# A transformer stack on one core: the gated product turned through memory, the mask in pieces, the mixer's end in another order

## The chip, the cores and the metric

The kernel runs on one core of one Trainium2 chip. The metric is the device time in microseconds (us). The kernel before takes 1723.46 us, the median of three runs (1722.71 to 1724.36).

## The reference

256 tokens of width 1024, all in fp32, pass through four layers. Two layers of the first kind:

```python
x = x + 0.5 * swiglu(rms_norm(x, ffn1_norm[l]), ffn1_w_in[l], ffn1_w_out[l])
x = x + mixer(rms_norm(x, mix_norm[l]), mix_w_in[l], ...)      # attention with a bias table, Fourier mix, two gates
x = x + 0.5 * swiglu(rms_norm(x, ffn2_norm[l]), ffn2_w_in[l], ffn2_w_out[l])
# swiglu: g, u = split(x @ w_in); (silu(g) * u) @ w_out, 2816 wide
```

and, after a norm, two of the second kind: a mixer of four groups (latent attention, short convolution, pooling, sliding-window attention), each group normalised by itself, scaled by `mix_norm` and projected by `w_o`, and then a gated FFN of the same size. There are six FFNs in all. A norm ends the stack. In the first kind's attention a table `rpb` is spread to a bias of 128 x (2 x 8 x 256), to which a mask (0 or -1e30) is added.

## The kernel before, in words

Tokens lie on partitions in two tiles of 128 (`t`). Every large product is done in three fp32r matmuls: both operands are split in a rounded part (`whi`, `xTh`, `bTh`) and a rest (`wlo`, `xTl`, `bTl`), and `product` adds high x high, high x low and low x high. Weights come in units of 1 MB (128 x 2048 fp32) through three slots of `raw`: SP loads a unit in two DMAs (`load`, when VectorE has split what was in the slot), ScalarE rounds it (`refill`, L671), VectorE subtracts (`refill`, L970). Units, steps and layers are counted by semaphores; each engine runs a list of its own, written out by hand, and nothing else orders the work.

An FFN has 11 steps of 256 hidden columns. A step of TensorE is `full_block` (48 matmuls of 512 columns: gate and up of step j+1 into the two banks `pg[1-par]`, weights in slots 2 and 0) and `down` (24 matmuls with the gated product of step j, weights in slot 1, summed in `acc`). ScalarE takes the silu (L701), VectorE multiplies (`product`, L1009) into `act`, tokens on partitions. `down` needs it with hidden columns on partitions: `turn` (L1451), four TensorE transposes into `pg[par][0]` between the two token tiles of `down`, then `product_hi` on ScalarE (L711) and `product_lo` on VectorE (L1019) split the result. VectorE's list for a step is: product_lo, refill slot 1, product of tile 0, refill slot 2, product of tile 1, refill slot 0; ScalarE's has the same order, with silu for the products.

SP's list of an FFN (L462 to L495) loads the first two units, then per step slots 2, 0 and 1. Between chosen steps of a layer's first FFN it issues other loads: the first gain, ahead of step 0; two gains and the constants ahead of step 2; the two gate biases ahead of step 4; the four pieces of the bias table ahead of step 6. GpSimd adds the mask to all of the bias in one instruction (L617) when all four have landed.

In the second kind's mixer (`mixer_b`) TensorE alternates half blocks of the input projection (i = 0 to 7) with small attention products. After the last one come the last attention product, `pair_T(0, 0)` and `pair_T(0, 1)` (transposes of the groups 2 and 3, scaled by VectorE in `scale_pair(0)`, L1287), the first half of the output projection with the convolution in it (`project`, `conv`), and the same for the groups 0 and 1.

Of the kernel before, what the change touches and what calls it, by code (L numbers as in the profile page):

```python
# [20 lines left out]
F32 = mybir.dt.float32  # L21
# [5 lines left out]
P = 128  # L27
# [34 lines left out]
B_IN = 1952  # L62

# [71 lines left out]
class Signals:  # L135

    def __init__(self, sem):
# [37 lines left out]
        self.act_ready = sem("act_ready")  # L176
        self.actT_tr = sem("actT_tr")
# [105 lines left out]
def build(nc, a, out):  # L283

    with ExitStack() as ctx:
# [23 lines left out]
        bTl = sb("bTl", [P, 8, T], F32R)  # L309
        gain_a = sb("gain_a", [P, D])  # L310
# [27 lines left out]
        sg, act = area(12288, TT, FB), area(12800, TT, FB)  # L338
        squared = area(12288, D)
# [47 lines left out]

        spread = nc.dram_tensor("rpb_spread", (GRID_W, DEPTH * NA_H, NA_DR * GRID_W), F32, kind="Internal").ap()
# [29 lines left out]
        def pair_bank(t):  # L418

            return (acc[2], pg[1][0])[t]  # L420
# [17 lines left out]
        def _(sp):  # L438
# [26 lines left out]
            def ffn(w_in, w_out, l, rnd, breaks=((0, None),)):  # L465
                def gate_up(slots, rnds, j):
                    for half in range(2):
                        at = l * (D * 2 * F) + half * (4 * P * 2 * F) + j * FB
# [19 lines left out]
            with sp.Fori(0, DEPTH) as l:  # L488
                (r1, _, _, _), (r2, _, _, _) = ffn_stages_a(l)
# [6 lines left out]
                def gains():  # L496
                    broadcast(gain_m[:, :], "mix_norm", l * D, D, s.gain_m_landed)
                    broadcast(gain_f[:, :], "ffn2_norm", l * D, D, s.gain_f_landed)
                    sp.dma_start(consts_a[:, :], a["consts_a"]).then_inc(s.consts_a_landed, 16)

                def gate_biases():
                    for t in range(TT):
                        broadcast(gate[:, t, :], "mix_gate_bias", l * 2 * D, 2 * D, s.gate_bias_landed)

                def attention_bias():
                    sp.wait_ge(s.rpb_spread, LOADED * NA_DR)
                    for t in range(TT):
                        for r in range(2):
                            first = GRID_H - 1 - (2 * t + r)
                            src = bass.AP(tensor=spread.tensor,  # L510
                                          offset=l * (NA_H * NA_DR * GRID_W) + first * GRID_W,
                                          ap=[[DEPTH * NA_H * NA_DR * GRID_W, GRID_W], [NA_DR * GRID_W, NA_H], [1, T]])
                            sp.dma_start(bias[GRID_W * r:GRID_W * (r + 1), t, :, :], src).then_inc(s.bias_landed, 16)
# [13 lines left out]
                ffn("ffn2_w_in", "ffn2_w_out", l, r2)  # L527
# [6 lines left out]
            with sp.Fori(0, DEPTH) as l:  # L534
# [26 lines left out]
                rf, _, _, _ = ffn_stage_b(l)  # L561
                ffn("w_gate_up_2", "w_down_2", l, rf)
# [15 lines left out]
        def _(pool):  # L578
# [33 lines left out]
            with pool.Fori(0, DEPTH) as l:  # L612
                norm(3 * l)
                pool.wait_ge(s.bias_landed, 64 * l + 64)
                pool.wait_ge(s.consts_a_landed, 16 * l + 16)
# [45 lines left out]
        def _(act_e):  # L661
# [35 lines left out]
            def ffn(rnd, f, n, o):  # L697
# [11 lines left out]
                def product_hi(j, par):  # L709
                    act_e.wait_ge(s.actT_tr, STEPS * f + j + 1)  # L710
                    act_e.activation(bTh[:, 2 * par:2 * par + 2, :], pg[par][0][:, :].rearrange("p (c n) -> p c n", c=2),  # L711
                                     ACT.Copy).then_inc(s.actT_hi, 1)

                with act_e.Fori(0, (STEPS - 1) // 2) as jj:
                    for par in range(2):
                        j = 2 * jj + par
                        product_hi(j, par)
                        refill(1, rnd + j + 1)
                        act_e.wait_ge(s.ffn_t0_done, STEPS * f + j + 2)
                        silu(0, 1 - par)  # L720
# [1174 lines left out]
```

## Time and profile before

| | us |
|---|---|
| median of the timed runs | 1723.46 (1722.71 to 1724.36) |
| span of the profiled execution, first to last instruction | 1721.5 |
| TensorE busy | 1671.8 (97%) |
| VectorE busy | 943.5 (55%) |
| ScalarE busy | 803.8 (47%) |
| GpSimd busy | 97.1 (6%) |
| mean granted TensorE clock | 0.990 of full |

The profile is of one execution. Its own time is the span and what lies around it (the start and end of the program, which the span leaves out); the timed runs are other executions, and their median is 2.0 us over the span. PE is TensorE, DVE is VectorE, ACT is ScalarE, POOL is GpSimd, SP is SyncE, whose only work is to issue DMAs. The granted clock is what share of full speed TensorE was given; 1.0 is 2.4 GHz and 0.5 is 1.2 GHz. A matmul's duration in the rows is longer than its distance to the next, since they are pipelined: distances between starts are what a matmul costs.

### The profile page before, as it was taken

How to read it: one execution, taken by the hardware profiler on the slowest of the kernel's cores; microseconds unless marked ns; L12 is line 12 of the kernel's file. 1: busy time of each engine (PE TensorE's matmuls, PEld its weight loads, DVE VectorE, ACT ScalarE, POOL GpSimd, SP SyncE). 2: the span in 40 equal slices, each digit the busy share in tenths (PEclk: the TensorE clock that was granted, in tenths of full speed). 3: DMA queues.
4: the chain of work that ended last, by engine and by line, in shares of the span. 5: the costliest groups of instructions: out<-in, count | busy, mean ns of one | idle time of the engine just before them, and what ended most of it. 6: DMA issues, size and time to landing. Idle time of an engine off the chain costs nothing.

```text
span 1721.5 us, 22066 instructions
## 1 busy us (share of the span) xinstructions
PE 1671.8 (97%) x7760; PEld 1376.7 (80%) x7760; DVE 943.5 (55%) x843; ACT 803.8 (47%) x899; POOL 97.1 (6%) x105
## 2 busy tenths in 40 slices
PE   6999999999999999999999999899999999999998
PEld 5887887888888787888888888787888878788886
DVE  4545545575545645465566545566554556665454
ACT  5443454544434543444455444465444446544443
POOL 2010000010000002000001000021100002110000
PEclk9999999999999999999999999999999999899999
DMA  8875453446565578555345655644456564336552
GB/s 259 295 221 175 172 190 123 139 156 199 176 208 188 175 251 240 174 173 181 111 152 166 203 188 194 240 127 129 141 190 200 179 195 144 125 127 201 189 192 89
DMA packets 209187, 308.96 MB, mean 179 GB/s; under 512 B 10400, under 2 KB 153504, under 8 KB 208480
## 3 DMA queue, kind: packets, MB, share of 16 engines
q1 hardware_dynamic: 208272, 305.18, 54.1%
q0 software_dynamic: 560, 1.84, 0.4%
q10 hardware_dynamic: 288, 1.05, 0.2%
q8 instruction: 43, 0.70, 0.2%
q14 instruction: 24, 0.20, 0.0%
HBM read 306.97 MB, written 2.88 MB: 180 GB/s over the span
## 4 chain that ended last, share of the span: by engine, by line
PE 90%; DVE 3%; ACT 3%; issue 2%; DMA 1%; POOL 1%; DVEq 0%; SPq 0%; ACTq 0%; POOLq 0%
PE pg L1380 19%; PE pg L1381 18%; PE pg L1382 18%; PE acc L1382 9%; PE acc L1380 9%; PE acc L1381 9%; PE pg L1451 2%; DVE wlo L970 2%; ACT whi L671 1%; DMA raw<-in_ffn_w_in 1%; PE pg L1393 1%; PE acc L1530 1%; PE acc L1550 1%; POOL ms L590 0%; PE acc L1538 0%
## 5 line engine op out<-in xcount | busy, mean ns | idle before, releaser
L970 DVE TENSOR_TENSOR wlo<-raw,whi 128x2048 fp32r<-128x2048 f32 x277 | 641.2, 2316 | 513.8 <-ACT whi L671 513.8
L671 ACT ACTIVATE whi<-raw 128x2048 fp32r<-128x2048 f32 x277 | 529.5, 1913 | 338.6 <-PE pg L1382 168.2
L1380 PE MATMUL pg<-whi,xTh 128*128 128x512 f32 (+1 forms) x1456 | 580.3, 399 | 9.9 <-DVE wlo L970 5.7
L1382 PE MATMUL pg<-whi,xTl 128*128 128x512 f32 (+1 forms) x1456 | 570.4, 392 | 0.0
L1381 PE MATMUL pg<-wlo,xTh 128*128 128x512 f32 (+1 forms) x1456 | 570.2, 392 | 0.0
L1380 PEld LDWEIGHTS pg<-whi,xTh 128*128 128x128 f32 x1456 | 276.3, 190 | 73.6 <-DVE wlo L970 9.8
L1382 PEld LDWEIGHTS pg<-whi,xTl 128*128 128x128 f32 x1456 | 276.0, 190 | 57.5
L1381 PEld LDWEIGHTS pg<-wlo,xTh 128*128 128x128 f32 x1456 | 276.5, 190 | 54.3
L1380 PE MATMUL acc<-whi,bTh 128*128 128x512 f32 (+1 forms) x572 | 229.6, 401 | 0.0
L1382 PE MATMUL acc<-whi,bTl 128*128 128x512 f32 (+1 forms) x572 | 224.3, 392 | 0.0
L1381 PE MATMUL acc<-wlo,bTh 128*128 128x512 f32 (+1 forms) x572 | 223.1, 390 | 0.0
L701 ACT ACTIVATE work<-pg,rstd 128x256 f32<-128x256 f32 x132 | 62.5, 474 | 234.8 <-PE pg L1382 234.7
L1382 PEld LDWEIGHTS acc<-whi,bTl 128*128 128x128 f32 x572 | 107.8, 188 | 23.5
L1381 PEld LDWEIGHTS acc<-wlo,bTh 128*128 128x128 f32 x572 | 108.1, 189 | 20.5
L1380 PEld LDWEIGHTS acc<-whi,bTh 128*128 128x128 f32 x572 | 107.8, 188 | 20.7 <-issue 0.6
L1009 DVE SCALAR_TENSOR_TENSOR work<-pg,rstd,work 128x256 f32<-128x256 f32 x132 | 63.5, 481 | 104.4 <-ACT work L701 104.4
L590 POOL TENSOR_TENSOR ms<-ss,eps 128x1 f32<-128x1 f32 x24 | 25.0, 1041 | 1202.7 <-ACT work L678 1202.6
L711 ACT ACTIVATE bTh<-pg 128x512 fp32r<-128x512 f32 x66 | 39.6, 599 | 83.7 <-PE pg L1451 83.7
L684 ACT ACTIVATE xTh<-pg 128x512 fp32r<-128x512 f32 x48 | 28.4, 597 | 64.6 <-PE pg L1393 64.5
L728 ACT ACTIVATE work<-acc 128x512 f32<-128x512 f32 (+2 forms) x44 | 25.2, 577 | 62.9 <-PE acc L1538 55.0
L1019 DVE TENSOR_TENSOR bTl<-pg,bTh 128x512 fp32r<-128x512 f32 x66 | 45.2, 684 | 15.2 <-ACT bTh L711 15.2
L1393 PE MATMUL pg<-ident,xn 128*128 128x128 f32 x192 | 30.2, 287 | 21.7 <-DVE xn L978 21.7
(159 smaller groups left out, 1048.2 us busy)
## 6 DMA issues: line engine op xcount, KB each, us to landing
raw<-in_ffn_w_in SPq DMA_DIRECT2D x176, 512.0 KB, 4.8
raw<-in_ffn_w_out SPq DMA_DIRECT2D x88, 512.0 KB, 4.0
raw<-in_w_gate_up SPq DMA_DIRECT2D x88, 512.0 KB, 4.7
raw<-in_mix_w_in SPq DMA_DIRECT2D x64, 512.0 KB, 4.1
raw<-in_w_down SPq DMA_DIRECT2D x44, 512.0 KB, 4.0
raw<-in_w_in SPq DMA_DIRECT2D x24, 512.0 KB, 4.8
raw<-in_mix_w_o SPq DMA_DIRECT2D x16, 512.0 KB, 4.7
raw<-in_w_o SPq DMA_DIRECT2D x16, 512.0 KB, 4.5
```

The costliest lines, as they stand in the source:

```text
L671: act_e.activation(whi[:, slot, :], raw[:, slot, :], ACT.Copy).then_inc(s.w_hi_ready, 1)
L684: act_e.activation(xTh[:, 4 * b:4 * b + 4, tok(t)], pg[b][t][:, :].rearrange("p (c n) -> p c n", c=4), ACT.Copy).then_inc(s.xT_hi_ready, 1)
L701: act_e.activation(sg[:, t, :], pg[par][t][:, 0:FB], ACT.Silu, scale=rstd[:, t:t + 1]).then_inc(s.silu_ready, 1)
L711: act_e.activation(bTh[:, 2 * par:2 * par + 2, :], pg[par][0][:, :].rearrange("p (c n) -> p c n", c=2), ACT.Copy).then_inc(s.actT_hi, 1)
L970: v.tensor_tensor(wlo[:, slot, :], raw[:, slot, :], f32(whi[:, slot, :]), ALU.subtract).then_inc(s.w_lo_ready, 1)
L1009: v.scalar_tensor_tensor(act[:, t, :], pg[par][t][:, FB:2 * FB], rstd[:, t:t + 1], sg[:, t, :], ALU.mult, ALU.mult).then_inc(s.act_ready, 1)
L1019: v.tensor_tensor(bTl[:, part, :], pg[par][0][:, :].rearrange("p (c n) -> p c n", c=2), f32(bTh[:, part, :]), ALU.subtract).then_inc(s.act ...
L1380: pe.matmul(dst, xh, wh, start=first and i == 0, stop=False)
L1381: pe.matmul(dst, xh, wl, start=False, stop=False)
L1382: mm = pe.matmul(dst, xl, wh, start=False, stop=last and i == len(pairs) - 1)
L1393: tr = pe.transpose(pg[b][t][:, c * P:(c + 1) * P], xn[:, t, at:at + P], ident[:, :])
L1451: tr = pe.transpose(pg[par][0][:, c * T + t * P:c * T + (t + 1) * P], act[:, t, c * P:(c + 1) * P], ident[:, :])
```

## The change

The gated product of the steps 1 to 9 is no longer turned by TensorE. VectorE transposes `act` in blocks of 32 x 32 within each band of 32 partitions (`turned`), ScalarE's queue stores the result in a DRAM tensor (one DMA, 128 rows of 2 KB), and SP's queue reads it back in four DMAs (32 partitions each, pieces of 512 bytes), so that the bands change places; with the blocks turned and the bands exchanged, `moved` holds the transpose. It is then split from SBUF as it was from PSUM. Steps 0 and 10 keep TensorE's `turn`. On SP the reads of a step stand between the loads of slot 2 and slot 0, and so do the other loads, one per step: first gain in step 0, `gain_m` in 2, constants in 3 (in the first layer only), the bias table's pieces in 4 to 7. The gate biases and `gain_f` are loaded in the mixer instead, and SP's loop over the two layers is written out. GpSimd adds the mask in 16 instructions of 256 columns. In `mixer_b` the end is put in another order: `sw_out(1)` and its square come before the pooling's; `scale_pair` is done per token tile; `pair_T(0, 0)` lies in the last half block and `pair_T(0, 1)` in the first projection, the last attention product behind it; units 13 and 14 are refilled together, ahead of the second pair's split; the first pair uses the banks `pg[1][0]` and `acc[1]`.

```diff
+        turned, moved = area(11264, TT * FB), area(11776, TT * FB)
+        act_blocks = act.rearrange("p t (c b j) -> p b (t c) j", c=2, b=QUADS)
+        turned_blocks = turned.rearrange("p (b n i) -> p b n i", b=QUADS, n=TT * 2)
+        moved_blocks = moved.rearrange("p (a e) -> p a e", a=QUADS)
+        moved_T = moved.rearrange("p (a n i) -> p n a i", a=QUADS, n=TT * 2)
+        stored = nc.dram_tensor("act_blocks", (QUADS, Q, QUADS, TT * FB // QUADS), F32, kind="Internal").ap()
-        def pair_bank(t):
-            return (acc[2], pg[1][0])[t]
+        def pair_bank(k, t):
+            return ((pg[1][0], acc[1]), (acc[2], pg[1][0]))[k][t]
...
@@ SP
+                def move(j):
+                    sp.wait_ge(s.act_stored, 16 * (TURNED * f + j))
+                    for b in range(QUADS):
+                        sp.dma_start(moved_blocks[Q * b:Q * (b + 1)], stored[:, :, b, :].rearrange("a j e -> j a e"))\
+                            .then_inc(s.act_moved, 16)
+                def step(j, moving, extra=None):
+                    def between():
+                        if moving:
+                            move(j - 1)
+                        if extra:
+                            extra()
+                    gate_up((2, 0), (rnd + j, rnd + j + 1), j + 1, between)
+                    down(1, rnd + j + 1, j)
                 gate_up((0, 1), (rnd, rnd), 0)
-                for (begin, other), (end, _) in zip(breaks, (*breaks[1:], (STEPS - 1, None))):
-                    if other:
-                        other()
-                    with sp.Fori(begin, end) as j:
-                        gate_up((2, 0), (rnd + j, rnd + j + 1), j + 1)
-                        down(1, rnd + j + 1, j)
+                for j in range(2):
+                    step(j, False, extras.get(j))
+                for j in range(2, max(extras, default=1) + 1):
+                    step(j, True, extras.get(j))
+                with sp.Fori(max(extras, default=1) + 1, STEPS - 1) as j:
+                    step(j, True)
                 down(2, rnd + STEPS - 1, STEPS - 1)
+                move(STEPS - 2)
...
-                ffn("ffn1_w_in", "ffn1_w_out", l, r1, ((0, gain), (2, gains), (4, gate_biases), (6, attention_bias)))
+                extras = {0: gain, 2: mixer_gain}
+                if l == 0:
+                    extras[3] = constants
+                for i in range(4):
+                    extras[4 + i] = lambda i=i: attention_bias(i // 2, i % 2)
...
                     block_units("mix_w_in", l, A_IN, 0, col, BANK, 2 * b, rm)
+                    if b < 2:
+                        gate_bias(b)
+                    if b == 3:
+                        ffn_gain()
@@ GpSimd
-                flat = bias.rearrange("p t h k -> p (t h) k")
-                pool.tensor_tensor(flat, flat, consts_a[:, CA_MASK:].unsqueeze(1).to_broadcast([P, TT * NA_H, T]),
-                                   ALU.add).then_inc(s.bias_masked, 1)
+                for t in range(TT):
+                    for h in range(NA_H):
+                        pool.tensor_tensor(bias[:, t, h, :], bias[:, t, h, :], consts_a[:, CA_MASK:], ALU.add).then_inc(s.bias_masked, 1)
@@ ScalarE, FFN
+                def moved_hi(j, par):
+                    act_e.wait_ge(s.act_moved, 16 * QUADS * (TURNED * f + j))
+                    act_e.activation(actTh[:, par].rearrange("p n (a i) -> p n a i", a=QUADS), moved_T,
+                                     ACT.Copy).then_inc(s.actT_hi, 1)
+                def store(j):
+                    act_e.wait_ge(s.act_turned, TURNED * f + j)
+                    act_e.dma_start(stored.rearrange("a j b e -> (a j) (b e)"), turned).then_inc(s.act_stored, 16)
...
+                with act_e.Fori(0, (STEPS - 3) // 2) as jj:
+                    for par in (1, 0):
+                        j = 2 * jj + 2 - par
+                        moved_hi(j, par)
+                        step(j, par)
+                        store(j + 1)
@@ ScalarE, mixer_b
                 group_square(0, 3, 0, s.sw_o_sb, 2 * l + 1)
+                group_square(1, 3, 1, s.sw_o_sb, 2 * l + 2)
                 refills(11)
...
                 mla_probs_T(1)
+                group_square(4, 0, 0, s.mla_o_sb, 2 * l + 1)
+                pair_hi(0, 0)
                 mla_exp(2)
                 out_gate_copy(1)
                 mla_probs_T(2)
                 pair_hi(0, 1)
+                refills(12)
...
-                refills(14)
+                refills(13, 14)
                 pair_hi(1, 0)
@@ VectorE, FFN
+                def moved_lo(j, par):
+                    v.wait_ge(s.actT_hi, STEPS * f + j + 1)
+                    hi, lo = (b[:, par].rearrange("p n (a i) -> p n a i", a=QUADS) for b in (actTh, actTl))
+                    v.tensor_tensor(lo, moved_T, f32(hi), ALU.subtract).then_inc(s.actT_lo, 1)
+                def step(j, par, turn=True):
+                    refill(1, rnd + j + 1)
+                    product(0, 1 - par, j + 1)
+                    refill(2, rnd + j + 1)
+                    product(1, 1 - par, j + 1)
+                    if turn:
+                        v.wait_ge(s.act_ready, 2 * STEPS * f + 2 * j + 4)
+                        v.transpose(turned_blocks, act_blocks).then_inc(s.act_turned, 1)
+                    refill(0, rnd + j + 2)
@@ VectorE, mixer_b
                 mla_out(0)
+                sw_out(1)
...
                 refills(11)
-                sw_out(1)
+                v.wait_ge(s.gain_m_landed, 16 * (DEPTH + 1) + 16 * l + 16)
+                scale_pair(0, 0)
                 mla_max(2)
+                scale_pair(0, 1)
+                pair_lo(0, 0)
+                conv_in(1)
+                pair_lo(0, 1)
                 refills(12)
-                conv_in(1)
-                v.wait_ge(s.gain_m_landed, 16 * (DEPTH + 1) + 16 * l + 16)
-                scale_pair(0)
                 mla_out(1)
-                pair_lo(0, 0)
-                pair_lo(0, 1)
-                refills(13)
...
-                scale_pair(1)
-                refills(14)
+                scale_pair(1, 0)
+                scale_pair(1, 1)
+                refills(13, 14)
                 pair_lo(1, 0)
@@ TensorE
-                        if t == 0:
-                            turn(j + 1, 1 - par)
+                        if t == 0 and last:
+                            turn(STEPS - 1, 0)
...
+                                    {0: sw_operands, 7: lambda: pair_T(0, 0)}.get(i))
...
                         mla_attend(0)
+                        sw_attend(2)
                         pool_mix()
...
-                mla_attend(2)
-                pair_T(0, 0)
-                pair_T(0, 1)
-                project(0, 0)
+                project(0, 0, lambda: pair_T(0, 1))
+                mla_attend(2)
                 conv()
                 project(0, 1)
```

## Rows read from the trace of the kernel before

**Rows 1.** The page: an engine's busy time; the chain of waits by engine.
```profile
PE 1671.8 (97%) x7760; PEld 1376.7 (80%) x7760; DVE 943.5 (55%) x843; ACT 803.8 (47%) x899; POOL 97.1 (6%) x105
...
PE 90%; DVE 3%; ACT 3%; issue 2%; DMA 1%; POOL 1%; DVEq 0%; SPq 0%; ACTq 0%; POOLq 0%
```

**Rows 2.** Timeline of TensorE, one step: start, us, line, operation, out<-in, count.
```profile
434.54 0.39 PE L1382 MATMUL pg<-whi,xTl 128*128 128x512 f32 x1
...
437.26 0.40 PE L1382 MATMUL acc<-whi,bTl 128*128 128x512 f32 x1
...
438.17 0.40 PE L1381 MATMUL acc<-wlo,bTh 128*128 128x512 f32 x1
```

**Rows 3.** Timeline of VectorE, same loop; in brackets: idle before, what ended it.
```profile
420.46 2.29 DVE L970 TENSOR_TENSOR wlo<-raw,whi 128x2048 fp32r<-128x2048 f32 x1 [0.40 <-ACT whi L671]
...
434.20 2.29 DVE L970 TENSOR_TENSOR wlo<-raw,whi 128x2048 fp32r<-128x2048 f32 x1 [3.68 <-ACT whi L671]
436.40 0.48 DVE L1009 SCALAR_TENSOR_TENSOR work<-pg,rstd,work 128x256 f32<-128x256 f32 x1
437.28 2.29 DVE L970 TENSOR_TENSOR wlo<-raw,whi 128x2048 fp32r<-128x2048 f32 x1 [0.40 <-ACT whi L671]
```

**Rows 4.** Timeline of ScalarE in the same step.
```profile
438.13 0.60 ACT L711 ACTIVATE bTh<-pg 128x512 fp32r<-128x512 f32 x1 [0.89 <-PE pg L1451]
440.99 1.92 ACT L671 ACTIVATE whi<-raw 128x2048 fp32r<-128x2048 f32 x1 [2.25 <-PE acc L1382]
```

**Rows 5.** Timeline of SP's DMA issues in the same step.
```profile
436.72 4.06 SPq L447 DMA_DIRECT2D raw<-in_ffn_w_in  x4
```

**Rows 6.** DMA issues by transfer: count, KB each, median us to landing.
```profile
raw<-in_ffn_w_in SPq DMA_DIRECT2D x176, 512.0 KB, 4.8
...
x<-in_x ACTq DMA_DIRECT2D x2, 512.0 KB, 4.9
...
out<-xn SPq DMA_DIRECT2D x2, 512.0 KB, 2.6
...
raw<-in_w_ukv SPq DMA_DIRECT2D x4, 128.0 KB, 2.1
```

**Rows 7.** Timelines of GpSimd, VectorE and TensorE at the mask; busy time by window.
```profile
120.87 9.03 POOL L617 TENSOR_TENSOR shared<-shared,consts_a 128x4096 f32<-128x4096 f32 x1 [94.78 <-DMA shared<-rpb_spread]
...
125.93 6.13 DVE L970 TENSOR_TENSOR wlo<-raw,whi 128x2048 fp32r<-128x2048 f32 x1 [3.68 <-ACT whi L671]
...
132.51 0.66 PE L1451 MATMUL pg<-ident,work 128*128 128x128 f32 x4 [3.13 <-DVE work L1009]
...
681.61 0.66 PE L1451 MATMUL pg<-ident,work 128*128 128x128 f32 x4 [2.27 <-DVE work L1009]
...
133.70:137.20 3.50, 3.50 (x10) 2.73 (x9) 1.55 (x2) 0.10 (x1) 0.00 (x0) 0.51 1.02 332
```

**Rows 8.** Timeline of TensorE near the end of the first `mixer_b`.
```profile
1193.14 1.10 PE L1724 MATMUL pg<-work 128*128 128x64 f32 x8 [0.69 <-ACT work L728]
1195.88 1.11 PE L1837 MATMUL acc<-ident,xn 128*128 128x128 f32 x4 [1.63 <-DVE xn L1287]
...
1198.48 0.79 PE L1380 MATMUL pg<-whi,xTh 128*128 128x512 f32 x1 [0.63 <-DVE xTl L1295]
...
1203.02 3.62 PE L1764 MATMUL pg<-work,shared 128*128 128x256 f32 x16
```

**Rows 9.** Timelines of SP and VectorE at the kernel's start; busy time by window.
```profile
1.26 2.27 SPq L447 DMA_DIRECT2D raw<-in_ffn_w_in  x4
3.71 0.93 SPq L455 DMA_DIRECT2D gain_a<-in_ffn_norm  x1
5.06 8.31 SPq L447 DMA_DIRECT2D raw<-in_ffn_w_in  x4
...
12.42 1.29 DVE L978 TENSOR_TENSOR xn<-x,gain_a 128x512 f32<-128x512 f32 x2 [0.19 <-DMA gain_a<-in_ffn_norm]
...
7.00:12.30 5.30, 0.00 (x0) 0.00 (x0) 2.29 (x1) 4.27 (x3) 0.72 (x1) 1.00 1.07 367
```

More of the change, by code:

```diff
@@ L62 @@
 B_IN = 1952
+Q = 32
+QUADS = P // Q
+TURNED = STEPS - 2
 FFN_ROUNDS = STEPS
@@ L309, in build @@
         bTl = sb("bTl", [P, 8, T], F32R)
+        actTh, actTl = (b[:, 0:4, :].rearrange("p (r c) (t i) -> p r (c t) i", r=2, t=TT) for b in (bTh, bTl))
         gain_a = sb("gain_a", [P, D])
@@ L463, in block_units, with ffn, gate_up @@
                          [rows(name, at + 2 * u * P * pitch, pitch, i % SLOTS, 2 * u * n, 2, n) for u in range(2)])
-            def ffn(w_in, w_out, l, rnd, breaks=((0, None),)):
-                def gate_up(slots, rnds, j):
+            def ffn(w_in, w_out, l, rnd, f, extras={}):
+                def gate_up(slots, rnds, j, between=None):
                     for half in range(2):
+                        if half == 1 and between:
+                            between()
                         at = l * (D * 2 * F) + half * (4 * P * 2 * F) + j * FB
@@ L727, in copy @@
+                product_hi(0, pg[0][0])
+                step(0, 0)
+                store(1)
+                with act_e.Fori(0, (STEPS - 3) // 2) as jj:
[4 more added lines that the diff above has]
+                        store(j + 1)
+                moved_hi(STEPS - 2, 1)
+                step(STEPS - 2, 1)
+                product_hi(1, pg[0][0])
             def copy(dst, src, sem, scale=1.0):
@@ L1450, in turn, with down @@
                         for c in range(2):
-                            tr = pe.transpose(pg[par][0][:, c * T + t * P:c * T + (t + 1) * P], act[:, t, c * P:(c + 1) * P], ident[:, :])
+                            tr = pe.transpose(pg[par][0][:, (2 * t + c) * P:(2 * t + c + 1) * P], act[:, t, c * P:(c + 1) * P], ident[:, :])
                     tr.then_inc(s.actT_tr, 1)
                 def added(t, par, slot, n2, k, first, last):
-                    return product(acc[2 * t + n2][:, :], [(bTh[:, 2 * par + k, tok(t)], bTl[:, 2 * par + k, tok(t)],
+                    return product(acc[2 * t + n2][:, :], [(actTh[:, par, 2 * t + k, :], actTl[:, par, 2 * t + k, :],
                                                             *weights(slot, k * D + n2 * BANK, BANK))], first=first, last=last)
-                def down(j, par, slot, r, first):
+                def down(j, par, slot, r, first, last):
                     pe.wait_ge(s.actT_lo, STEPS * f + j + 1)
@@ L1484, in last_down, with step @@
                                     transposes(0, n2, o + 1)
-                def step(j, par, amid=None, first=False):
+                def step(j, par, amid=None, first=False, last=False):
                     full_block((2, 0), (rnd + j, rnd + j + 1), BANK, pg[1 - par], s.ffn_t0_done, amid=amid)
-                    down(j, par, 1, rnd + j + 1, first)
+                    down(j, par, 1, rnd + j + 1, first, last)
                 step(0, 0, {(0, 1): lambda: turn(0, 0)}, first=True)
@@ L1493, in ffn @@
                     step(2 * jj + 2, 0)
-                step(STEPS - 2, 1)
+                step(STEPS - 2, 1, last=True)
                 last_down(2, rnd + STEPS - 1)
@@ L1786, in pool_mix, with pair_T @@
                     mm.then_inc(s.unit_done, 1)
+                def pair_T(k, t):
+                    half = 1 - k
+                    if k == 0 and t == 0:
+                        pe.wait_ge(s.z_ready, 2 * l + 1)
+                        pe.wait_ge(s.out_gate_sb, 2 * l + 1)
+                    if k == 0 and t == 1:
+                        pe.wait_ge(s.sw_biased, 3 * l + 3)
+                    pe.wait_ge(xn_ready[t], 2 * (o + 1) + k + 2)
+                    for c in range(4):
+                        at = (4 * half + c) * P
+                        tr = pe.transpose(pair_bank(k, t)[:, c * P:(c + 1) * P], xn[:, t, at:at + P], ident[:, :])
+                    tr.then_inc(s.tr_done, 1)
                 for i in range(8):
@@ L1825, in mixer_b @@
                         mla_probs_T(2)
-                mla_attend(2)
-                def pair_T(k, t):
-                    half = 1 - k
-                    if k == 0 and t == 1:
-                        pe.wait_ge(s.z_ready, 2 * l + 1)
-                        pe.wait_ge(s.out_gate_sb, 2 * l + 1)
-                    pe.wait_ge(xn_ready[t], 2 * (o + 1) + k + 2)
-                    for c in range(4):
-                        at = (4 * half + c) * P
-                        tr = pe.transpose(pair_bank(t)[:, c * P:(c + 1) * P], xn[:, t, at:at + P], ident[:, :])
-                    tr.then_inc(s.tr_done, 1)
                 def project(i, t, amid=None):
```

124 lines of the change are left out of this document (57 added, 67 removed).

## The prediction

> **What bounds the kernel now.** I read first the page's busy shares and its chain of waits [rows 1]: TensorE is busy for 1671.8 of 1721.5 us and carries 90% of the chain that ended last. So a part of the change can only gain by taking work off TensorE, or by filling one of the places where TensorE stands idle or runs at half clock; and it can only lose by making TensorE wait. Then the timeline of one step of an FFN loop. 66 of these steps (11 in each of 6 FFNs) make up two thirds of the span. VectorE's splits of the same slot lie 16.82 us apart (420.46 and 437.28) [rows 3]; that is the period. TensorE's 72 large matmuls in it (48 for gate and up, 24 for down) follow each other by 0.2267 us (12 of them from 434.54 to 437.26) [rows 2], 16.32 us in all. What is left, 0.50 us, is the four transposes of the gated product: from 437.26 to 438.17 pass 0.91 us for two matmuls and four transposes, 0.46 more than two matmuls [rows 2]; the other 0.04 is spread over the matmuls behind them. No engine makes TensorE wait in this loop. Last I looked for TensorE's idle places: beside the start there are two where the mask is added [rows 7] and one near each end of the second block's two mixers [rows 8].
>
> **The change, part by part.** The profile's span is 1721.5 us; the median of the timed runs, 1723.46, is 2.0 above it. I take the changes from the span and add these 2.0, so they come off the median as they are.
>
> *Transposes removed.* Products 1 to 9 of each FFN go through memory, 0 and 10 stay on TensorE: 9 x 6 = 54 of 66 turns go. 54 x 0.50 = 27.0 us, if the way through memory is hidden.
>
> *Is it hidden?* The step becomes a ring that must close within 16.32 us: VectorE's product of token tile 1, block transpose, store, four reads, ScalarE's rounding copy, ScalarE's split of slot 1 (which stands behind that copy in its order and so waits for the reads), VectorE's split of slot 1, product of tile 0, split of slot 2, and then the next product of tile 1. Its terms:
> - product 0.48 [rows 3].
> - block transpose of 128x512: no such row; two VectorE operations of 512 elements take 1.29 [rows 9], one of 256 takes 0.48 [rows 3]; so between 0.5 and, at two passes, 1.4; I take 0.7.
> - store of 256 KB on ACT's queue: 512 KB of output land in 2.6 with nothing beside them, 512 KB of x on this same queue in 4.9 beside weight loads [rows 6]. The store runs beside the load of slot 2, issued at the same moment [rows 5]; between 2.0 and 4.9, I take 3.0.
> - SP wakes 0.23 after what it waits for (434.20 + 2.29 = 436.49 [rows 3], issue at 436.72 [rows 5]).
> - four reads of 64 KB: four issues took 2.27 in a row [rows 9], so the last is issued 1.7 after the first and lands 2.1 later, as the 128 KB loads do [rows 6]: 3.8; at worst, behind what is left of slot 2's megabyte in the same queue, 6.5.
> - rounding copy 0.60, split on ScalarE 1.92 [rows 4], two splits of 2.29 and a product of 0.48 on VectorE [rows 3], each beginning some 0.09 before the end of the one ahead: 7.2.
> - semaphores between engines, about 0.2.
> Sum 0.48 + 0.7 + 3.0 + 0.23 + 3.8 + 7.2 + 0.2 = 15.6, with 14.4 and 20.9 as ends. So 0.7 us are spare, and TensorE alone should set a period of 16.32. Its own deadline is later still: it needs slot 1 split when the down matmuls begin, some 1.3 us after VectorE is through, and that is spent once in an FFN, not in each step; a ring of up to 16.46 would cost nothing over nine steps.
>
> A rule of the Trainium skill speaks against it: DMA: Bandwidth & Descriptors, section on the anatomy of one DMA, says that a transfer's fixed cost is mostly the wait for the receipt of the last write, and that this is longest when the target is HBM; its latency table gives HBM 0.2 us on average and 2 us at high load. The one store in this trace lands fast, but with no other traffic [rows 6]; beside traffic no row shows a store. By the rows the store's term is 3.0 and the ring 15.6; by the rule at high load it would be some 5 and the ring 17.6, 0.8 over the period before.
>
> *What waits behind the new waits.* On ScalarE the wait for the reads holds up the split of slot 1 and the silu of tile 0, and VectorE waits for both: that is the ring. On SP the wait for the store holds up the loads of slots 0 and 1. VectorE's transpose stands ahead of the split of slot 0, which then ends 0.7 us later; TensorE needs it only at the second half of the next block, over 3 us after 439.57 [rows 3], so nothing. SP's load of slot 0 now stands behind its wait for the store and four issues: it is issued about 6 us after the product instead of 3.4, and lands about 4.8 us after that [rows 6], where ScalarE wants it at 15.3; 4 us spare, less in the four steps that also load a bias piece. The extra traffic, 0.5 MB beside 3 MB in a step, needs 3.5 MB in 16.3 us, 215 GB/s, where 367 GB/s have been moved [rows 9]. Cost nothing; without that cover the same 54 steps pay for it.
>
> *Mask in pieces.* One GpSimd addition of 4096 elements takes 9.03 us, and VectorE's split of 2.29 that meets it takes 6.13 [rows 7]: they exclude each other. TensorE stands for 3.13, and then runs 8 matmuls at 0.427 instead of 0.227 while the clock is at half (the window 133.70 to 137.20 shows 0.51, 1.2 GHz, after that idle place), 1.6 us; in the other layer 2.27 [rows 7]. Together 7.0. A piece of 256 elements should take 9.03/16 = 0.56, with some overhead 0.7, and holds one split by at most that. The 16 pieces reach over one step or a bit more, two splits of the ring in it: up to 1.4 us against 0.7 + 1.3 spare. I take 0.5 per layer as lost: gain 6.0, between 3 and 7.
>
> *Mixer end.* In each of two layers TensorE waits 0.69 for the last probabilities, 1.63 for the scaled pair and 0.63 for its split, then works at half clock: 12 matmuls from 1198.48 to 1203.02 take 4.54 where 2.72 are needed, and the eight transposes lose some 0.8 [rows 8]. 2.95 + 1.8 + 0.8 = 5.6 per layer. Now the pair's squares and scaling come before the last scores, its transposes lie inside matmul blocks, and the last attention follows the first projection. Following the new orders with the durations of rows 3, 4 and 8, the first projection finds its operand about 0.3 us ahead. But the second pair's split now stands behind two weight splits of 2.29 on VectorE, and TensorE then waits about 1.1 there. 5.6 - 1.1 = 4.5 per layer, 9.0 for two; between 0 (a new idle place brings the half clock back) and 12.
>
> *Loads moved.* Only one lies bare: at the start the gain of the first norm was issued at 3.71, ahead of slot 2's megabyte at 5.06; now it is behind it in the same queue. VectorE's first use, at 12.42, waited for exactly this load [rows 9]. A megabyte at the 367 GB/s of that stretch [rows 9] is 2.9 us; x's second half and the bias table's loads share the engines then, so I take 3.7, between 2.5 and 5, and TensorE's whole start shifts by it. In the second layer the same gain lands some 4 us before it is wanted. Gate biases and constants move to where the queue has room: nothing.
>
> Sum: -27.0 - 6.0 - 9.0 + 3.7 = -38.3; 1723.5 - 38.3 = 1685.
>
> **Rivals.**
> A. *The ring is a bit too long*, between 16.46 and 17.0: the reads queue behind slot 2's load. For it: that load's landings and the reads fall together; 0.7 is not much. Against: each term was taken in company. At 16.8 TensorE's saving is given back wholly: 1685 + 27 = 1712.
> B. *The trip through memory decides* (the other side): store and reads together take 2.5 us longer than the 7.0 I gave them, as x's 4.9 in rows 6 and reads at their worst would have it. The ring is 18.1, each of 54 steps loses 1.3 against before: +70, with the other parts 1723.5 + 70 - 11.3, and less what the first steps of each FFN have spare (some 6 x 1.3 = 8): 1774. It decides from a ring of 17.0 on: there 54 x 0.2 = 11 eat the other gains. For it: 2.0 to 4.9 for the store. Against: 4.9 was measured for twice the bytes. The section of the Trainium skill named above would have the store go this way.
> C. *Only the transposes count*: the mixer end gives nothing, since TensorE meets the new idle place and the half clock again, and the mask in pieces costs as much as whole: 1723.5 - 27 + 3.7 = 1700. For it: the reordered work is the same on VectorE and ScalarE. Against: the waits that go are covered by matmuls that exist.
>
> **How the numbers follow.** Forecast 0.60 (1676 to 1694), A 0.12, B 0.16, C 0.12. The range that holds 8 in 10 leaves out B and a little below: 1675 to 1716. No change means within 0.2%, 3.4 us, about what a measurement of this kernel can tell. Faster: forecast, C and most of A, less a little for a ring near 17: 0.82. Same 0.03. Slower 0.15.
>
> **What would show it.** In the changed profile: period between two splits of a slot 16.3 (16.8 or more under A, 18 under B); before ScalarE's rounding copy a wait of some 6 us for the reads, and none of TensorE for the split of slot 1; VectorE's new operation near 0.7; the store landing about 3.0 after issue, the last read about 3.8 after the first; GpSimd with 16 short additions a layer and TensorE without an idle place there; VectorE's first use of the gain near 16 instead of 12.42; near the mixers' end one wait of about 1 us in place of three, and no stretch at half clock. The forecast is wrong if TensorE waits in the loop each step, or if the start does not move.

## The result: 34.5 us slower, and the profile after

The changed kernel takes 1757.6 us (median of four runs, 1756.5 to 1758.8) against 1723.1 of the kernel before on the same chip (1720.7 to 1724.4): 1.0200 times as long, with a 95% interval of 1.0186 to 1.0215. I had forecast 1685, with 1675 to 1716 as range. The span of the profiled execution is 1756.8, 35.3 more than before.

The page of the profile after, busy times, the chain of waits, and two of the DMA issues:

```profile
PE 1661.1 (95%) x7544; PEld 1352.2 (77%) x7544; DVE 966.6 (55%) x897; ACT 782.7 (45%) x899; POOL 113.6 (6%) x135
PE 37%; DMA 24%; DVE 14%; issue 10%; ACT 8%; SPq 4%; POOL 1%; ACTq 0%; DVEq 0%; POOLq 0%
...
act_blocks<-work ACTq DMA_DIRECT2D x54, 256.0 KB, 5.5
work<-act_blocks SPq DMA_DIRECT2D x216, 64.0 KB, 2.0
```

TensorE has 216 instructions less, as meant (54 x 4), and is busy for 10.7 us less. But the chain that ended last, 90% TensorE before [rows 1], is 37% TensorE now. The rest runs through the store, the reads, SP, ScalarE and VectorE: the ring of the prediction has become what bounds the loop. The waits name its places (engine and line, what it waited for: us in total, times, longest):

```profile
ACT bTh L758 <- DMA work<-act_blocks: 551.6, 54, 11.6
DVE bTl L1084 <- ACT bTh L758: 400.1, 54, 8.3
PE acc L1455 <- DVE wlo L1030: 43.8, 50, 1.8
```

ScalarE's wait for the reads would harm nobody by itself. The third row does: TensorE waits 50 times for VectorE's split of slot 1, and that split stands behind the moved product.

One turn of the ring, from the timelines of VectorE, ScalarE, SP and TensorE (start, us, line, operation; idle before in brackets):

```profile
443.29 0.48 DVE L1069 SCALAR_TENSOR_TENSOR work<-pg,rstd,work 128x256 f32<-128x256 f32 x1
443.56 0.95 SPq L462 DMA_DIRECT2D raw<-in_ffn_w_in  x2
443.81 0.71 DVE L1094 STREAM_TRANSPOSE work<-work 128x512 f32<-128x512 f32 x1
444.55 0.33 ACTq L773 DMA_DIRECT2D act_blocks<-work  x1
450.04 1.76 SPq L499 DMA_DIRECT2D work<-act_blocks  x4
453.44 0.63 ACT L758 ACTIVATE bTh<-work 128x512 fp32r<-128x512 f32 x1 [10.66 <-DMA work<-act_blocks]
453.98 1.90 ACT L714 ACTIVATE whi<-raw 128x2048 fp32r<-128x2048 f32 x1
455.92 2.29 DVE L1030 TENSOR_TENSOR wlo<-raw,whi 128x2048 fp32r<-128x2048 f32 x1 [1.11 <-ACT whi L714]
458.26 0.50 PE L1455 MATMUL acc<-whi,bTh 128*128 128x512 f32 x1 [0.81 <-DVE wlo L1030]
460.72 0.48 DVE L1069 SCALAR_TENSOR_TENSOR work<-pg,rstd,work 128x256 f32<-128x256 f32 x1
461.23 0.71 DVE L1094 STREAM_TRANSPOSE work<-work 128x512 f32<-128x512 f32 x1
```

From one block transpose to the next are 17.42 us, where the period before was 16.82 and I had forecast a ring of 15.6. The terms, forecast and measured: product 0.48 and 0.52; transpose 0.7 and 0.74; **store 3.0 and 5.49** (444.55 to 450.04, the issue of the reads included, so 0.23 of waking is in it); reads 3.8 and 3.40; from the copy to the next product 7.2 and 7.28. Only the store is far off: with SP's waking on both sides 3.23 were forecast and 5.49 measured, 2.3 us more. It also lies above the upper end that I had kept, 4.9.

I read the rest from TensorE's timeline, by the starts of the first and the last turn on TensorE (steps 0 and 10) in each of the six FFNs. In us, with the experiments told below:

```
stretch                  before   after   turns on TensorE  split first  combined  loop written out
start to first turn       35.13   37.81       38.85            37.52       34.20       34.55
FFN 1 (mask)             166.23  167.87      161.40           156.87      156.90      156.90
FFN 2                    161.40  167.40      161.27           156.88      156.88      156.90
layer 1 to layer 2        29.84   34.36       31.38            32.99       33.79       28.90
FFN 3 (mask)             163.80  166.53      161.38           156.90      156.90      156.90
FFN 4                    161.40  166.65      161.38           156.88      156.88      156.90
first mixer_b            141.64  146.01      138.90           146.06      138.10      138.90
FFN 5                    161.38  166.65      161.38           156.87      156.87      156.88
second mixer_b           138.46  136.06      135.08           134.62      133.68      133.95
FFN 6                    161.26  166.29      161.38           156.88      156.88      156.87
```

(The mixers of the first kind, 192.5 in all columns, and the end, 16.0, are left out.) An FFN without the mask takes 161.38 before. The six loops together take 1001.4 after against 6 x 161.38 = 968.3: the ring costs 33.1. The mask's stalls, 7.2 in the two loops that had them, are gone. The start costs 2.7 (this stretch moves by itself: 35.13, 34.98 and 33.69 in three profiles in which nothing was changed there), the passage to the second layer 4.5, the first `mixer_b` 4.4; the second gives 2.4 back. 33.1 - 7.2 + 2.7 + 4.5 + 4.4 - 2.4 = 35.1 of the 35.3.

### The profile page after: what moved, and what is told of

Read it like the earlier page. It is cut to its first block, busy times and chain, and to the rows that moved or that the text cites. A ratio compares the mean times of both kernels' runs of the same rounds, so it can differ in the third digit from the quotient of the medians.

```text
span 1756.8 us, 21384 instructions
## 1 busy us (share of the span) xinstructions
PE 1661.1 (95%) x7544; PEld 1352.2 (77%) x7544; DVE 966.6 (55%) x897; ACT 782.7 (45%) x899; POOL 113.6 (6%) x135
## 4 chain that ended last, share of the span: by engine, by line
PE 37%; DMA 24%; DVE 14%; issue 10%; ACT 8%; SPq 4%; POOL 1%; ACTq 0%; DVEq 0%; POOLq 0%
DMA act_blocks<-work 17%; DVE wlo L1030 8%; PE pg L1455 8%; PE pg L1457 7%; PE pg L1456 7%; ACT whi L714 7%; DMA work<-act_blocks 6%; SPq L499 4%; PE acc L1455 3%; PE acc L1457 3%; PE acc L1456 3%; DVE work L1069 2%; DVE work L1094 2%; PE pg L1468 1%; PE acc L1605 1%
## 5 line engine op out<-in xcount | busy, mean ns | idle before, releaser
L1030 DVE TENSOR_TENSOR wlo<-raw,whi 128x2048 fp32r<-128x2048 f32 x277 | 632.4, 2284 | 204.9 <-ACT whi L714 204.9
L758 ACT ACTIVATE bTh<-work 128x512 fp32r<-128x512 f32 x54 | 34.1, 632 | 551.6 <-DMA work<-act_blocks 551.6
L1084 DVE TENSOR_TENSOR bTl<-work,bTh 128x512 fp32r<-128x512 f32 x54 | 40.2, 745 | 400.1 <-ACT bTh L758 400.1
```

What stands on the lines that cost most here:

```text
L758: act_e.activation(actTh[:, par].rearrange("p n (a i) -> p n a i", a=QUADS), moved_T, ACT.Copy).then_inc(s.actT_hi, 1)
L1030: v.tensor_tensor(wlo[:, slot, :], raw[:, slot, :], f32(whi[:, slot, :]), ALU.subtract).then_inc(s.w_lo_ready, 1)
L1084: v.tensor_tensor(lo, moved_T, f32(hi), ALU.subtract).then_inc(s.actT_lo, 1)
```

## Experiments: what the ring costs, and where it can be opened

**All but the way through memory.** The changed kernel with `turn`, `product_hi` and `product_lo` of the kernel before, and without the block transpose, the store and the reads:

```diff
-                        moved_hi(j, par)
+                        product_hi(j, par)
...
-                        if t == 0 and last:
-                            turn(STEPS - 1, 0)
+                        if t == 0:
+                            turn(j + 1, 1 - par)
```

> The changed kernel with the gated product turned by TensorE again in every step, as before; mask in pieces, spread loads, mixer end and the other load order stay. Theory (the trip through memory is what costs: period 17.43 instead of 16.82): all six FFN loops are back at 161.4 us from the first to the last turn, the two idle places at the mask stay away (-7), the mixer end keeps its 8, the late gain keeps costing 4.2 and 4.5: about 1719, between 1714 and 1726. Rival (the moved loads, the pieces of the mask and the mixer end do the harm): some 1745 to 1757.

1715.1 us (0.9949 of before, 0.9932 to 0.9967): the other parts gain some 8, and the trip through memory costs 42.5 against this run. All loops are at 161.3 to 161.4, so the stalls at the mask stay away. The first `mixer_b` gains 2.7 here and loses 4.4 in the changed kernel. That loss comes with the trip too, but not with the longer period: in the next run the period is TensorE's own, and the stretch is still 146.06.

**The order that closes the ring.** On ScalarE and VectorE slot 1 is split before the moved product is taken (`step` began with this `refill` and leaves it out now):

```diff
+                        refill(1, rnd + j + 1)
                         moved_hi(j, par)
-                        step(j, par)
+                        step(j, par, False)
```

> The changed kernel with one place in two lists exchanged: ScalarE and VectorE split slot 1 before they take the moved product, no longer behind it. The store stays as it is. Theory (the ring closes through that order; the store's 5.5 us alone would harm nobody, as TensorE needs the moved product only 16 us after the last gate-and-up matmul): the period falls from 17.43 to 16.32, 54 x 1.11 = 60 less: 1698, between 1690 and 1706, with the store still at 5 to 6 us. Rival 1 (the 0.5 MB of extra traffic or the queues hold up the weights themselves): period 17 or more, over 1735. Rival 2 (the store grows when the loads come earlier, and the product arrives late): TensorE waits for the product's split, between 1706 and 1735.

1696.3 us (0.9849, 0.9833 to 0.9866), 61 less than the changed kernel; 60 were expected. VectorE's splits of slot 1, then ScalarE's copy, the store and the split, in the middle of the second FFN:

```profile
418.10 2.29 DVE L1033 TENSOR_TENSOR wlo<-raw,whi 128x2048 fp32r<-128x2048 f32 x1 [1.18 <-ACT whi L714]
434.42 2.29 DVE L1033 TENSOR_TENSOR wlo<-raw,whi 128x2048 fp32r<-128x2048 f32 x1 [2.64 <-ACT whi L714]
...
429.64 0.33 ACTq L774 DMA_DIRECT2D act_blocks<-work  x1
432.47 1.92 ACT L714 ACTIVATE whi<-raw 128x2048 fp32r<-128x2048 f32 x1 [3.24 <-PE acc L1463]
438.32 0.63 ACT L758 ACTIVATE bTh<-work 128x512 fp32r<-128x512 f32 x1 [3.93 <-DMA work<-act_blocks]
```

434.42 - 418.10 = 16.32, TensorE's own 72 x 0.2267. The trip is as slow as ever (the store's median is 5.5 again), but the split of slot 1 now runs at 432.47, while the store is under way, and waits for TensorE instead of the reads. A stall of 10.66 ahead of the copy has become one of 3.93, and it delays nothing. So the slow store alone was not the loss. It became one because an operation which had no need of it stood behind it.

**The store with nothing ahead of it.** ScalarE's and VectorE's lists are as in the changed kernel; SP's wait for the store and its four reads stand ahead of the load of slot 2:

```diff
                     def between():
-                        if moving:
-                            move(j - 1)
                         if extra:
                             extra()
+                    if moving:
+                        move(j - 1)
                     gate_up((2, 0), (rnd + j, rnd + j + 1), j + 1, between)
```

> The changed kernel with one place in SP's list exchanged: the four reads (and the wait for the store) stand ahead of the load of slot 2, no longer behind it, so that the store has no megabyte issued at the same moment. ScalarE's and VectorE's lists stay. Theory A (the store waits beside SP's loads): it lands in 2.6 to 3.5 us instead of 5.5, the ring is 14.9 to 15.4 and the period 16.32: about 1698. Theory B (a store to memory costs 5 us with its receipt, whatever runs beside): store 5 to 5.5, period 17.3 or more, 1750 to 1770. In between: slot 1's megabyte alone still holds it up, store 4 to 4.5, ring 16.3: 1698 to 1712.

1702.1 us (0.9878, 0.9862 to 0.9895). The DMA issues (KB each, median us from issue to landing):

```profile
act_blocks<-work ACTq DMA_DIRECT2D x54, 256.0 KB, 2.0
work<-act_blocks SPq DMA_DIRECT2D x216, 64.0 KB, 2.0
```

2.0 instead of 5.5, so a store to memory with its receipt is not slow in itself. Four of the loops run at 156.9 or 157.3; the two with bias loads take 158.3 and 159.3. The store is not the reason, it takes 2.6 to 3.0 in those steps. The weights of slot 0 now stand behind a bias piece: ScalarE waits 2.7 to 3.8 us for them, and TensorE three times for their split, 0.46 to 1.35 us.

**Order of issue, or queue?** In the run above the last load, slot 1's, had been issued 6 us ahead of the store. Two more runs keep slot 2's megabyte close by; slot 1's load lies 3.6 us ahead of the store in both, as in the changed kernel. In one, SP issues the store itself, ahead of that load:

```diff
+                    if moving:
+                        store(j - 1)
                     gate_up((2, 0), (rnd + j, rnd + j + 1), j + 1, between)
```

> The changed kernel with the store issued by SP, ahead of the load of slot 2 in the same queue, instead of by ScalarE just behind it; reads stay behind that load. Nothing is left out, and the load of slot 2 still follows within 1 us. Theory A (transfers are served in the order of their issue, and the store waited for the megabyte issued ahead of it): the store lands in 2.0 to 3.0 us. Theory B (the engines' time is shared between what is in flight, whoever came first): 4 to 5.5 us. The reads come behind slot 2's megabyte by A, and take 4 to 5 instead of 3.3 if it is not through by then; the time lies between 1700 and 1757 by A, at 1757 by B.

In the other the store stays on ScalarE's queue, and the load is held back until the same moment:

```diff
+                    if moving:
+                        sp.wait_ge(s.act_turned, TURNED * f + j - 1)
                     gate_up((2, 0), (rnd + j, rnd + j + 1), j + 1, between)
```

> The changed kernel with one wait more on SP: the load of slot 2 is issued when VectorE has turned the blocks, that is at the moment of the store (ScalarE's queue, 0.0 to 0.2 us apart) instead of 1 us ahead of it. Both queues stay as they are. Issued by SP ahead of the load, the store landed in 2.2 us; that leaves open whether its order or SP's queue made it fast. Theory A (the order of issue decides, whatever the queue): it lands in 2.0 to 3.5 us. Theory B (ScalarE's queue comes behind SP's on the DMA engines): it stays at 4.5 to 5.5. Period by A 16.3 (the ring then has 15.5 or less) to 16.9, time 1700 to 1730; by B 17.4, 1757.

The DMA issues of the first and of the second, and the issues of one step of the second:

```profile
act_blocks<-work SPq DMA_DIRECT2D x54, 256.0 KB, 2.2
work<-act_blocks SPq DMA_DIRECT2D x216, 64.0 KB, 4.2
```

```profile
act_blocks<-work ACTq DMA_DIRECT2D x54, 256.0 KB, 2.5
work<-act_blocks SPq DMA_DIRECT2D x216, 64.0 KB, 3.8
```

```profile
432.05 0.33 ACTq L776 DMA_DIRECT2D act_blocks<-work  x1
432.34 0.99 SPq L462 DMA_DIRECT2D raw<-in_ffn_w_in  x2
435.36 1.76 SPq L499 DMA_DIRECT2D work<-act_blocks  x4
```

Theory A, twice: of the store and slot 2's load, what is issued first goes first, on either queue. 0.3 us ahead of the load the store takes 2.5; 1 us behind it, in the changed kernel, 5.5. The changed kernel's packets say the same. For 443.5 to 447.4 and for 447.4 to 449.6 the view of the DMA queues shows (q1 is SP's, q10 is ScalarE's; packets, MB, share):

```profile
q1 hardware_dynamic: 799, 1.21, 94.3%
```

```profile
q1 hardware_dynamic: 432, 0.42, 54.4%
q10 hardware_dynamic: 143, 0.26, 30.9%
```

The store was issued at 444.55, and in the first 2.85 us not one of its packets moved. Then they moved beside the load's last 0.42 MB, so the order is not strict. Why the two queues do not alternate from the start, no run shows. What the store gained in these two runs the reads partly lost: 4.2 and 3.8 instead of 2.0 each, behind the same megabyte. The block transposes are then 16.9 us apart in the mean in the first and 16.7 in the second (16.0 to 18.4 and 15.8 to 17.6), still over TensorE's 16.32, and the time 1725.4 for the first (one run) and 1712.3 for the second (0.9946, 0.9927 to 0.9966). With reads and store both ahead of the load, the ring is open.

## Experiments: the other parts

**The mask in pieces, alone** on the kernel before (the `for t`, `for h` loop of the change, and the count that waits for it; the bias loads stay together).

> The kernel before with the mask added in 16 pieces and nothing else; the four loads of the bias stay together ahead of step 6. From the run with TensorE's turns: the two FFN loops with the mask fell from 166.23 and 163.80 to 161.4. Theory (the pieces alone do it): 7.2 less than before, 1715 to 1716. Rival (the spread loads do part of it, or many short additions hold VectorE up as much as one long): 0 to 4 less.

1715.3 us (0.9961, 0.9948 to 0.9974): 7.1 less. FFN 1 and FFN 3 take 161.3 and 161.4. The pieces do it all, wherever the loads stand. In the changed kernel a layer's 16 pieces look so:

```profile
L661 POOL TENSOR_TENSOR shared<-shared,consts_a 128x256 f32<-128x256 f32 x16 | 15.9, 1027 | 118.7 <-DMA shared<-rpb_spread 118.7
```

15.9 us in all against 9.03 for the one instruction [rows 7], and yet, here and in the run with TensorE's turns, the loops with the mask are as long as the others.

**The mixer's end, alone** on the kernel before (the three lists of `mixer_b` and `pair_bank`).

> The kernel before with the mixer's end in the new order on TensorE, ScalarE and VectorE, and nothing else. My prediction gave it 4.5 per layer, 9.0. The milestones of the run with TensorE's turns give 2.7 and 3.4, but hold the moved loads of the mixer too. Theory (idle places gone, half clock shortened and not gone): 6 less, 1716 to 1718. Rival (the 4.5 per layer are there, and the moved loads ate part): 9 less, 1714.

1713.8 us (0.9952, 0.9936 to 0.9968), 8.7 less, which looks like my 9.0 and is not. The two mixers give 3.3 each (141.64 to 138.34, 138.46 to 135.12), 6.6 together. Most of the rest of the 10.4 by which this span is shorter lies elsewhere: 2.6 in FFN 1, where the mask's stall came this time without the half clock that followed it before [rows 7], and 0.9 in the passage to layer 2. Both sides of that are in the trace, and neither is the mixer's.

**Two orders of loads**, on top of the order that opens the ring: a layer's first gain ahead of slot 2's load again, and in `mixer_b` the first units of weights ahead of the gains and of the 2 MB of constants.

```diff
+                if 0 in extras:
+                    extras[0]()
...
+                block_units("w_in_2", l, B_IN, 0, 0, C_COLS, 0, rm)
                 broadcast(gain_a[:, :], "attn_norm_2", l * D, D, s.gain_a_landed)
-                block_units("w_in_2", l, B_IN, 0, 0, C_COLS, 0, rm)
+                if l == 0:
+                    sp.dma_start(consts_b[:, 0:CB_COLS], a["consts_b"]).then_inc(s.consts_b_landed, 16)
```

> The order of the run before last (slot 1 split ahead of the moved product), and two load orders: the first gain of a layer ahead of slot 2's load in step 0 again, and at the second block's mixers the weights of the first product ahead of the gains and of the 2 MB of constants. Theory (these two orders cost 4.2 + 4.5 at the two layer starts and 4.4 at the first mixer): 1698 - 13 = 1685, the start's first use of the gain back at 12.4. Rival (the losses at those places follow from the ring and went with it): no more than 3 below the run with the order alone, 1695 to 1700.

1684.8 us (0.9782, 0.9766 to 0.9798). The start gives 3.3, the first mixer 8.0 and not 4.4. What happened there, in the changed kernel, on SP, ScalarE, VectorE and TensorE:

```profile
1115.94 0.43 SPq L499 DMA_DIRECT2D work<-act_blocks  x1
1116.42 0.43 SPq L470 DMA_DIRECT2D gain_m<-in_final_norm  x1
1116.89 0.43 SPq L575 DMA_DIRECT2D shared<-in_consts_b  x1
1117.66 0.34 SPq L470 DMA_DIRECT2D gain_a<-in_attn_norm  x1
1118.30 1.11 SPq L462 DMA_DIRECT2D raw<-in_w_in  x2
...
1129.43 1.91 ACT L714 ACTIVATE whi<-raw 128x2048 fp32r<-128x2048 f32 x1 [6.52 <-DMA raw<-in_w_in]
1133.58 0.68 DVE L1078 TENSOR_TENSOR bTl<-pg,bTh 128x512 fp32r<-128x512 f32 x1
1134.39 0.79 PE L1455 MATMUL acc<-whi,bTh 128*128 128x512 f32 x1 [5.22 <-DVE bTl L1078]
```

SP holds the next stage's loads until the last product's store has landed. Then three megabytes of gains and constants go ahead of slot 0's weights, which land 11 us after their issue; ScalarE's split of slot 0 stands ahead of the last product's, and TensorE stands 5.22. Its clock is at half from 1133.2 to 1140.0. The passage to layer 2, however, did not move (32.99 and 33.79): the gain's load was not its cause.

**VectorE's loop over the layers.** What was it then? VectorE at that passage, in the changed kernel, and the instruction queue in its stretch of the DMA view (573 to 579 and 574 to 579):

```profile
574.51 0.69 DVE L1049 SCALAR_TENSOR_TENSOR x<-acc,x 128x512 f32<-128x512 f32 x1 [0.67 <-PE acc L1457]
577.82 1.29 DVE L1038 TENSOR_TENSOR xn<-x,gain_a 128x512 f32<-128x512 f32 x2 [2.62 <-issue]
```

```profile
q14 instruction: 2, 0.02, 1.3%
```

2.62 us idle with nothing to wait for ("issue"), between the end of one pass of the loop and the start of the next, while code is being loaded. The gain had been issued 11.7 us earlier, and the row names no DMA. The same place before had no gap. All six profiles with VectorE's changed FFN in this loop have one, of 2.45 to 2.73 us; the kernel before and the three runs with its old FFN have none. In the changed kernel TensorE stood 4.09 there, and its clock was at half from 576.8 to 587.1. The experiment writes this loop out on top of the last run:

```diff
-            with v.Fori(0, DEPTH) as l:
+            for l in range(DEPTH):
                 (first, second) = ffn_stages_a(l)
```

> The combined version (slot 1 split first, gain and mixer weights early) with VectorE's loop over the two layers of the first kind written out. In the combined version VectorE stands 2.84 us at the jump back to the loop's start (0.2 in the kernel before), and TensorE stands 4.39 there where it stood 1.81 before, with half clock for 6.8 us instead of 3.4. Theory (the jump over the now longer body is what the second layer's start lost, not the gain's load): the jump's 2.8 us go, TensorE stands 1.8 to 2.3 there, and the time falls by 2.6 to 4.3, to some 1681. Rival (straight code has to be fetched as well, or the next engine is late there): no change, 1684 to 1686.

(In the kept profile of the run that it starts from, VectorE's gap is 2.53 and TensorE's 4.01.)

1680.3 us (five runs, 1679.9 to 1682.0; 0.9758, 0.9738 to 0.9778), the fastest of all, 42 less than before and 77 less than the changed kernel. The passage takes 28.90 instead of 33.79, VectorE goes straight on, and no half clock follows:

```profile
549.82 0.69 DVE L1056 SCALAR_TENSOR_TENSOR x<-acc,x 128x512 f32<-128x512 f32 x1 [0.67 <-PE acc L1467]
550.42 1.28 DVE L1045 TENSOR_TENSOR xn<-x,gain_a 128x512 f32<-128x512 f32 x2
551.16 1.04 PE L1478 MATMUL pg<-ident,xn 128*128 128x128 f32 x6 [1.38 <-DVE xn L1045]
```

The Trainium skill has this case (Runtime: NRT & Kernel Launch, section on instruction fetch mechanics): code is fetched ahead in sequence only, and a taken branch to a page that is not held makes the engine wait for the fetch. The traces agree: 2.6 us at the jump where VectorE's loop body had grown, nothing where it was shorter or written out. How long a body may be no run here shows.

## Why the prediction was wrong

- *The step that failed* is "store of 256 KB on ACT's queue ... between 2.0 and 4.9, I take 3.0". With the 0.23 of SP's waking it was to be 3.23 and measured 5.49. These 2.3 us more, less 0.6 for shorter reads and for semaphores, lift the ring from 15.6 to 17.4. I wrote that the store "runs beside the load of slot 2, issued at the same moment". It is issued 1 us behind that load, and comes behind its megabyte. My own rows had that order: product at 436.40, 0.48 and 0.7 for it and the transpose, so a store at about 437.6, against the load at 436.72 [rows 3, rows 5]. The row of x on this same queue, 4.9 [rows 6], I discounted for having twice the bytes, as if a transfer's own size set its time. It is the middle of two loads of one size, the first issued at 1.07, just ahead of SP's weights, the second at 8.02, behind them. The DMA view of the kernel before for 0 to 5 and for 5 to 12 us has them apart:

```profile
x<-in_x ACTq DMA_DIRECT2D x1, 512.0 KB, 3.3
...
x<-in_x ACTq DMA_DIRECT2D x1, 512.0 KB, 6.4
```

  The one behind other loads took 3.1 us more. The chain that I drew for the ring was right. My point of no gain (a ring of 17.0) was not put to the test: the one ring over it is 17.42, and it lost.
- *Rival B* is what happened: a ring longer than before through the trip to memory. I gave it 0.16, though its deciding term had a like row at 4.9. Its price was worked out for a ring of 18.1; at 17.43 the same sum gives 54 x 0.61 = 33 and 1723.5 + 33 - 11 = 1745, and the last two points below are the other 12. The measurement decides against its reason here: with nothing ahead the store lands in 2.0, its receipt from memory included, and with the megabyte right behind it in 2.5.
- *Transposes removed*: right. A loop falls from 161.38 to 156.88 once the ring is open, 9 x 0.50.
- *The reads* (3.8): 3.4, right, by luck in part: the store ahead of them had already waited the megabyte out. Where it had not, each read took 3.8 or 4.2 instead of 2.0.
- *Mask in pieces*: 7.2 for 6.0, right in mechanism; the 0.5 per layer that I kept back was not lost.
- *Mixer's end*: the three idle places are gone and one of 0.77 is there, where I had forecast about 1.1. It gave 6.6 for 9.0. I had forecast no stretch at half clock, but each mixer still has one, now earlier: in the changed kernel the granted clock is 0.51 from 1215.1 to 1218.6, behind 24 matmuls of 64 columns at full clock, and seven matmuls there cost 0.2 us more each, 1.4 in all.
- *Start*: the gain's first use is at 16.61 (forecast: near 16), and the run with TensorE's turns pays 3.7 there, as forecast; 2.7 in the changed kernel.
- *Second layer*, "the same gain lands some 4 us before it is wanted": the gain did no harm, but 4.5 were lost there to VectorE's jump, which I had not thought of. I counted instructions that run, not the length of the code.
- *First `mixer_b`*, forecast as nothing: 146.01 against 138.34 with the mixer's new end alone, 7.7 lost, and the two orders of loads gave 8.0 back. I had listed that loads queue behind SP's wait, but looked at the loop only and not at what follows the last step.

Had the split of slot 1 stood ahead of the moved product, the store's 5.5 would have cost nothing, and the kernel would have taken the 1696.3 of that run, 11 above my forecast; the last two points make up most of these 11.

## What to carry to other kernels

When a round trip is put into an in-order list, ask first what stands behind its wait and has no need of it. Moving that ahead made the loop indifferent to a store of 5.5 us, where shortening the store mended it only in part. Price a transfer by what is issued ahead of it, on the other queue too, and not by its own bytes alone, and look at the stage boundaries too, where a wait on SP holds up the next stage's loads. A longer loop body can cost at the jump back though every instruction in it is hidden.

## Not expected of the hardware

- Two queues did not share the DMA engines packet by packet at once: issued 1 us behind 1 MB on SP's queue, a 256 KB store on ScalarE's queue moved no packet for 2.85 us and landed after 5.5; 0.3 us ahead of it, after 2.5; with nothing ahead, after 2.0.
- VectorE's block transpose of 128x512 fp32 takes 0.71 us, as long as a plain operation of that size (0.69).
- VectorE's jump back over the long loop body cost 2.45 to 2.73 us in six profiles; written out, nothing.
